# HGRN output from packed score blocks, and a new order of the scan's queues

## The reference, cut to what matters

```
diff = bi[..., :, None, :] - bi[..., None, :, :]
decay = jnp.exp(jnp.where(causal, diff, -jnp.inf))
scores = jnp.einsum("bhtd,bhsd,bhtsd->bhts", qi, ki, decay)
o = (jnp.einsum("bhts,bhsv->bhtv", scores, vi)
     + jnp.einsum("bhtd,bhdv->bhtv", qi * jnp.exp(bi), state))
```

## Time and profile before

| what | value |
|---|---|
| median of 3 executions | 1441.62 us (1437.52 to 1441.77) |
| the profiled execution | 1439.57 us, of which the span of its core is 1437.5 us |
| busy share of the span: PE, DVE, ACT, POOL | 97%, 70%, 48%, 14% |
| TensorE clock granted over the span | 0.988 of full |
| the scan | from 417.8 us to 575.9 us of the span |

### The profile page before, as it was taken

One profiled execution on the slowest core, in us unless ns is written; L12 is line 12 of the kernel. 1 busy time (PEld: TensorE's weight loads), 2 busy tenths in 40 slices (PEclk: granted clock), 3 DMA queues, 4 the chain that ended last, 5 costly groups with the idle time before them and its releaser, 6 DMA issues.

```text
span 1437.5 us, 22414 instructions
## 1 busy us (share of the span) xinstructions
PE 1398.9 (97%) x8579; PEld 1166.2 (81%) x8579; DVE 999.3 (70%) x1508; ACT 696.5 (48%) x1344; POOL 199.0 (14%) x225
## 2 busy tenths in 40 slices
PE   9999999999988888999999999999999999999998
PEld 7877888888877777878888888888888888888886
DVE  7584545561136777367897999999999575577567
ACT  6443456411366776256674343334444444454455
POOL 4000001101036655010000000000000144400000
PEclk9999999999998999999999999999999999999999
DMA  9642334446523433544442334335326766424213
GB/s 260 81 73 30 45 88 123 156 104 106 150 82 104 123 105 95 181 141 154 147 135 87 109 103 165 100 116 176 118 74 240 251 191 197 140 89 132 88 59 147
DMA packets 157866, 181.96 MB, mean 127 GB/s; under 512 B 25849, under 2 KB 96703, under 8 KB 157760
## 3 DMA queue, kind: packets, MB, share of 16 engines
q1 hardware_dynamic: 157760, 180.53, 43.3%
HBM read 130.43 MB, written 49.28 MB: 125 GB/s over the span
## 4 chain that ended last, share of the span: by engine, by line
PE 88%; DVE 4%; ACT 2%; DMA 2%; issue 2%; SPq 2%; DVEq 0%; ACTq 0%
PE psum L2538 9%; PE psum L2539 9%; PE psum L2540 9%; PE psum L2477 5%; PE psum L2479 5%; PE psum L2478 5%; PE psum L678 4%; PE psum L680 4%; PE psum L679 4%; PE psum L2450 4%; PE psum L2451 4%; PE psum L2452 4%; PE psum L736 3%; PE psum L738 3%; PE psum L737 3%; PE psum L1398 2%
## 5 line engine op out<-in xcount | busy, mean ns | idle before, releaser
L166 DVE TENSOR_TENSOR w_wlo<-w_raw,w_whi 128x1024 fp32r<-128x1024 f32 x66 | 87.8, 1332 | 231.9 <-ACT w_whi L151 231.7
L151 ACT ACTIVATE w_whi<-w_raw 128x1024 fp32r<-128x1024 f32 x66 | 69.7, 1059 | 177.0 <-PE psum L2452 80.2
L3271 DVE TENSOR_TENSOR g_slot<-w_raw,g_slot 128x512 fp32r<-128x512 f32 x77 | 62.5, 812 | 65.3 <-ACT g_slot L2845 65.3
L678 PE MATMUL psum<-h_hi,w_whi 128*128 128x512 f32 x256 | 100.7, 393 | 0.0
L680 PE MATMUL psum<-h_hi,w_wlo 128*128 128x512 f32 x256 | 99.7, 390 | 0.0
L679 PE MATMUL psum<-h_lo,w_whi 128*128 128x512 f32 x256 | 99.7, 389 | 0.0
L2845 ACT ACTIVATE g_slot<-w_raw 128x512 fp32r<-128x512 f32 x77 | 48.7, 632 | 104.8 <-PE psum L2479 99.6
L2450 PE MATMUL psum<-w_whi,m_hi 128*128 128x512 f32 x224 | 88.2, 394 | 0.9 <-DVE w_wlo L166 0.9
L2451 PE MATMUL psum<-w_wlo,m_hi 128*128 128x512 f32 x224 | 87.3, 390 | 0.0
L2452 PE MATMUL psum<-w_whi,m_lo 128*128 128x512 f32 x224 | 87.2, 389 | 0.0
L3529 POOL TENSOR_TENSOR mixed_home<-mixed_home 128x512 f32<-128x512 f32 x11 | 14.7, 1344 | 507.7 <-DMA mixed_home<-in_w_down 506.4
(11 more groups left out here) (463 smaller groups left out, 3883.1 us busy)
## 6 DMA issues: line engine op xcount, KB each, us to landing
w_raw<-in_w_up SPq DMA_DIRECT2D x39, 512.0 KB, 3.9
w_raw<-in_w_in SPq DMA_DIRECT2D x36, 512.0 KB, 6.3
s_rows<-pair_work SPq DMA_DIRECT2D x11, 1024.0 KB, 4.2
w_raw<-s_rows SPq DMA_DIRECT2D x44, 256.0 KB, 2.7
g_rows<-pair_work SPq DMA_DIRECT2D x18, 512.0 KB, 2.6
w_raw<-g_rows SPq DMA_DIRECT2D x33, 256.0 KB, 3.1
w_raw<-in_w_out SPq DMA_DIRECT2D x16, 512.0 KB, 4.5
mixed_home<-in_w_down SPq DMA_DIRECT2D x32, 256.0 KB, 3.4
```

Source lines behind the costliest of these rows:

```text
L678: pe.matmul(out, wh[:, w], self.hi[:, kt, part], start=(kt == 0), stop=False)
```

## The change

1. `s_h_scores`, the clearing of it, the second `s_h_near` buffer and `sp_unpack` with its 32 DMAs go. The HGRN output of a head is summed straight from the packed blocks: 4 products of 32 x 32 blocks on the diagonal, 2 of 32 x 32 blocks off it, 1 of a 64 x 64 block (`s_h_far`), and the product with the state as before.
2. The last level's decay is made like the others: one `dve_differ` (128 x 512) and two ACT exponentials, in place of eight small ones.
3. The order of all four queues is new. On PE, `pe_hgrn` of chunk c moves from the end of chunk c into the beginning of chunk c+1, `pe_solve` and `pe_outputs` move forward, score 7 moves behind `mix_g`, dt32 and dx. DVE, ACT and SP follow.
4. `hd` moves from bank 3 to bank 1, and `mix_g` from bank 2 to bank 7.

```diff
-    BANK_OF = {"ks": 2, "solve": 3, "gd": 3, "og": 4, "oh": 5, "hd": 3, "turn": 2, "mix_g": 2, "mix_h": 5,
+    BANK_OF = {"ks": 2, "solve": 3, "gd": 3, "og": 4, "oh": 5, "hd": 1, "turn": 2, "mix_g": 7, "mix_h": 5,
...
         out = self.banks.open(pe, ("oh", c), self.BANK_OF["oh"])
+        near, far = self.near_heads(), self.packed(self.far)
         for h in range(NH):
-            if c:
-                pe.matmul(hs(out, h), hs(self.hqd, h), hs(self.hstate, h), start=True, stop=False)
-            ins = pe.matmul(hs(out, h), hs(self.sc, h), hs(self.hv, h), start=(c == 0), stop=True)
-        self.multiplied.mark(ins, ("oh", c))
+            for b in range(P // SB):
+                rows = slice(b * SB, (b + 1) * SB)
+                ins = pe.matmul(hs(out, h)[rows, :], near[rows, h, 0:SB], hs(self.hv, h)[rows, :], start=(h == 0), stop=False,
+                                skip_group_check=True)
+        self.multiplied.mark(ins, ("oh", c, 0))
+        if c:
+            for h in range(NH):
+                pe.matmul(hs(out, h), hs(self.hqd, h), hs(self.hstate, h), start=False, stop=False, skip_group_check=True)
+        self.done(pe, ("oh", c, 0))
+        for h in range(NH):
+            for b in range(0, P // SB, 2):
+                keys, queries = slice(b * SB, (b + 1) * SB), slice((b + 1) * SB, (b + 2) * SB)
+                ins = pe.matmul(hs(out, h)[queries, :], near[keys, h, SB:2 * SB], hs(self.hv, h)[keys, :], start=False, stop=False,
+                                skip_group_check=True)
+        self.multiplied.mark(ins, ("oh", c, 1))
         if c < NT - 1:
             self.banks.released(pe, ("turn", c))
             self.pe_products(pe, ("hd", c), self.BANK_OF["hd"], lambda h: hs(self.hkd, h), lambda h: hs(self.hv, h))
+        self.done(pe, ("oh", c, 1))
+        for h in range(NH):
+            ins = pe.matmul(hs(out, h)[P // 2:P, :], far[0:P // 2, h, :], hs(self.hv, h)[0:P // 2, :], start=False,
+                            stop=(h == NH - 1), skip_group_check=True)
+        self.multiplied.mark(ins, ("oh", c))
...
         for c in range(NT):
             more = c + 1 < NT
+            if c:
+                self.pe_hgrn(pe, c - 1)
             self.pe_score(pe, c, 2)
             if c:
                 self.pe_dt64(pe, c)
             self.pe_score(pe, c, 3)
+            if c:
+                self.pe_solve(pe, c)
...
```

More of the change, by code:

```diff
@@ L1275, in __init__ @@
             self.ed, self.ql, self.kl = k.ed, k.ql, k.kl
-            self.sc, self.hqd, self.hkdt, self.hkd, self.hstate, self.hv = (
-                t("h_" + n) for n in ("scores", "qd", "kdt", "kd", "state", "v"))
+            self.sc_gap, self.hqd, self.hkdt, self.hkd, self.hstate, self.hv = (
+                t("h_" + n) for n in ("gap", "qd", "kdt", "kd", "state", "v"))
             self.gate = [t("h_gate"), t("g_gate")]
             self.on = t("normed", DM)
-            self.near = [t(f"h_near{i}", DG // 2) for i in range(2)]
-            self.middle = t("h_middle", NT * NH)
+            self.near, self.far = t("h_near", DG // 2), t("h_far", DG // 2)
             self.junk = t("junk", P, mybir.dt.bfloat16)
@@ L1307, in near_part, with near_heads @@
         return ap[:, at:at + NH * width].rearrange("p (h t) -> p h t", h=NH)
[L1309 to L1310 removed]
+    def near_heads(self):
+        return self.near[:].rearrange("p (h t) -> p h t", h=NH)
     def packed_blocks(self, ap, m):
@@ L1349, in load_rows @@
         sp.dma_start(tile[:], self.front.rows_out[c * P:(c + 1) * P, at:at + DG]).then_inc(self.s[name + "_in"], 16)
-    def sp_unpack(self, sp, c):
-        self.banks.released(sp, ("score", c, LEVELS - 1))
-        self.banks.released(sp, ("near", c))
-        if c:
[L1356 to L1360, removed]
     def sp(self, sp):
@@ L1534, in pe_hgrn @@
         pe.wait_ge(s["v_in"], (c + 1) * 16)
-        pe.wait_ge(s["unpacked"], (c + 1) * (P // SB) * 16)
-        self.banks.released(pe, ("score", c, LEVELS))
+        for n in (LEVELS - 1, LEVELS):
+            self.banks.released(pe, ("score", c, n))
+        self.banks.released(pe, ("near", c))
         if c:
@@ L1577, in pe @@
                 self.pe_dx(pe, c + 1)
-            self.pe_hgrn(pe, c)
+            self.pe_score(pe, c, 7)
+            if more:
+                self.pe_ks(pe, c + 1)
             self.pe_score(pe, c + 1, 0)
@@ L1602, in act_exp @@
         ed = self.ed[n % 3]
-        if lv in (0, LEVELS - 1) and n >= 3:
+        if lv == 0 and n >= 3:
             act.wait_ge(self.s["levels"], n - 2)
@@ L1608, in act_exp @@
                                  scale=-1.0, bias=1.0)
[L1609 to L1615, removed]
         else:
-            act.wait_ge(self.s["differed"], c * self.NEAR + lv)
+            act.wait_ge(self.s["differed"], c * (LEVELS - 1) + lv)
             act.activation(side(ed[:], 0), side(ed[:], 0), ACT.Exp, scale=-1.0)
@@ L1777, in dve_near @@
         self.done(dve, ("score", c, self.NEAR))
-        if c >= 2:
-            dve.wait_ge(self.s["unpacked"], (c - 1) * (P // SB) * 16)
-        bank, blocks = self.banks.of(("near", c)), self.near_heads(c)[:, :, 0:SB]
+        if c:
+            self.done(dve, ("oh", c - 1))
+        bank, blocks = self.banks.of(("near", c)), self.near_heads()[:, :, 0:SB]
         for n in range(self.NEAR + 1):
@@ L1800, in dve_place @@
         data = self.packed(self.banks.of(key))[0:P - ahead, :, 0:ahead]
[L1801 to L1806, removed]
+        if c:
+            self.done(dve, ("oh", c - 1))
+        here = self.packed(self.far)[0:ahead] if n == LEVELS else self.near_heads()[0:P - ahead, :, SB:2 * SB]
+        ins = dve.tensor_copy(here, data)
         self.banks.release(ins, key)
@@ L1887, in dve @@
         self.dve_rhs(dve, 0)
[L1888 to L1891, removed]
+        dve.memset(self.near[:], 0.0).then_inc(s["cleared"], 1)
         self.front.finished(dve)
@@ L1912, in dve @@
             self.dve_place(dve, c, 6)
+            if more:
+                self.dve_state(dve, c)
+            self.dve_query(dve, c)
             if c:
@@ L1916, in dve @@
                 self.slabs.remainder(dve, self.front.first["q"] + NH + 1)
[L1917 to L1921, removed]
             self.dve_dt(dve, c + 1, 0)
+            self.dve_dx(dve, c + 1)
             if c:
                 self.dve_mix(dve, c - 1, 1)
+            self.dve_differ(dve, c + 1, 2)
+            self.dve_place(dve, c, 7)
         self.dve_outputs(dve, NT - 1)
```

53 lines of the change are left out of this document (21 added, 32 removed).

## The result

The changed kernel takes 1468.03 us (median of 4, 1466.17 to 1470.11) against 1441.69 before: ratio 1.0189, 95% interval 1.0165 to 1.0214, slower by 26 us. The sign was forecast, the size was not: 12 us were predicted, and the time lies just above the range of 1438 to 1468 us.

A forecast was written before the change was run, and what follows sets the result against it. A ring of handoffs, not one full engine, was taken to bound the kernel. Six chunks +5.8, first -1.3, last +3.1, clock +4.5 gave +12.1 on 1441.62: 1453.7 us, range 1438 to 1468.

The forecast's parts named there:

- The ring: Handoffs between PE and DVE in each chunk: a DVE leg of 11.9 us plus a PE leg of 9.0 us.
- The products: HGRN output with hd on PE from packed blocks: diagonal tiles run at once, 4.95 us a chunk at full clock.
- the serial tiles: Rival: PE's diagonal tiles run one after another, +29 us over eight chunks, 1482 us; chance 0.10.
- The full-clock chunk: Each of six chunks takes 20.9 us against 19.94 before, +5.8 us in all.
- DVE's leg: From dt64's end on PE to DVE's release of mix_g: 11.9 us of handoff and DVE work per chunk.
- The clock term: PE's two idle times per chunk bring the lower clock in every second chunk, 1.5 us each: +4.5, between 0 and +9.
- The ends: First chunk -1.3 us, as its DMA wait goes; last chunk +3.1 us, 15.7 from dt64 to the end against 12.6.
- PE with its wait for y32 alone: Rival: bank 7 is free in time, a chunk is PE's own work plus 1.35 us, 19.3; 1439 us, chance 0.15.
- PE alone as the bound: Rival: PE has neither wait and stays at the upper clock, 17.9 us a chunk, 1429 us; chance 0.11.
- Part 2: Last level's decay as one DVE difference and two ACT exponentials: +0.65 us on DVE's path, ACT's saved 2 us bring nothing.

The follow-up runs named there:

- the bank number: The changed kernel with mix_g in bank 0 instead of bank 7, so score 7 need not wait for its release: 1444.66 us, ratio 1.0019.
- parts 1 and 2 in the old order: The kernel before with packed HGRN output and the last decay as one difference and two exponentials, queues and banks as before: 1433.46 us, ratio 0.9954.
- the gap filled: The changed kernel with mix_g's four transposes issued three times in chunks 1 to 6, occupying PE ahead of dt32: 1456.88 us, ratio 1.0118.
- the packed output alone: The kernel before with HGRN output from packed blocks and no unpacking DMAs, every queue and bank as before: 1432.36 us, ratio 0.9937.
- the new order without the difference: The changed kernel with mix_g in bank 0 and eight small ACT exponentials again in place of the DVE difference: 1443.18 us, ratio 1.0009.
- outputs first: The changed kernel with mix_g in bank 0 and DVE's outputs of the chunk before placed ahead of its HGRN state update: 1443.01 us, ratio 1.0011.

## Why the prediction was wrong, point by point

**The ring is right.** Where each chunk would wait, for whom and how long came as told: 1.7 us before score 7 for `mix_g`, about a microsecond before dt32, no wait for the unpacking DMAs. DVE's idle time before the copy of dt64 was 5.8 us, 3 forecast. That the bank clash makes the loss is shown by the bank number: without it the loss is gone. That the rest of the new order costs too is shown by parts 1 and 2 in the old order, 11 us below.

**The products are right.** 5.19 us measured at the full clock for the output with hd, 4.95 forecast, 8.5 for the serial tiles. The four 32 x 32 tiles on the diagonal do run at once with 128 columns and one bank:

```profile
461.32 1.08 PE L1531 MATMUL psum<-s_h_v,s_h_near 32*32 32x128 f32 x32
462.33 1.16 PE L1536 MATMUL psum<-s_h_state,s_h_qd 128*128 128x128 f32 x8
```

32 records in 1.01 us, and 0.9 was taken; one after another they would need 3.6 by the forecast's estimate. The rule on row tiles and banks of the Trainium skill ("TensorEngine Tiling (Array Packing)", "Restrictions and Gotchas") would have given that. The measurement decides against it for tiles that differ in row and column both.

**The full-clock chunk was sized 0.7 too short.** 20.9 forecast, 21.62 measured with the gap filled. I followed score 7's bank to its last user and not og's. Bank 4 is free only after DVE's outputs, which the new order puts behind the state update, so og, `mix_h` and score 6 come later, and DVE then waits 0.77 us for score 6, a wait that was not in its leg:

```profile
497.09 0.68 DVE L1766 TENSOR_TENSOR s_h_ed<-hgrn_f 128x512 f32<-128x512 f32 x1
498.55 0.29 DVE L1797 COPY s_h_near<-psum 96x128 f32<-96x128 f32 x1 [0.77 <-PE psum L1465]
```

DVE's leg with its handoff was 12.58 (490.50 to 503.08), 12.0 forecast; the output's 0.24 makes it 0.8, a little more than the 0.7 to be explained. Over six chunks 4.3 us.

**The clock term failed.** This is the step of the prediction that failed; the sizes of the ring above and of the ends below add to it. It took every second chunk at 1.5 us: +4.5, at most +9. From dt64 to dt64 the six chunks took 140.9 us, 23.5 each; less 21.62 that is 1.9 a chunk, 11 us. Every one of the six had a low stretch, and in the last three it was about twice as long (a clock of 0.85 and 0.86 over a chunk, and 0.93 and 0.94 in two of the others). Even the upper end allowed for one stretch per chunk like those of before, and no more. "Every second" was low by what lay on record, too: the forecast set one gap of 2.17 us that was not followed by the lower level against one of 3.10 that was, but another gap of 2.17 in the same trace was followed by it:

```profile
455.87 0.46 PE L1542 MATMUL psum<-s_h_state,s_h_qd 128*128 128x128 f32 x2 [2.17 <-DMA s_h_scores<-s_h_near]
...
457.34 0.63 PE L1542 MATMUL psum<-s_h_state,s_h_qd 128*128 128x128 f32 x2
```

Five of the six outputs from 455.87 to 555.40 had the lower level behind them (clock 0.90 to 0.92 up to the next output); five of six at 1.5 would have been +7.5. Why the stretches of the changed kernel are longer stays open. Two gaps stand close together there, and with the first one nearly filled the time fell by 11 us; but a gap of about a microsecond without the wait for `mix_g` is followed by the lower level as well, in five of six chunks of one kernel and in one of six of another. So it is open what sets the length.

**The ends.** First chunk -1.3 forecast, +0.9 measured (dt64 of chunk 1 ends at 444.53, 443.68 before, though the scan began 0.4 us earlier), with a low stretch of 13.7 us where before had two, of 6.8 and of 3.6. Last chunk +3.1 forecast, +7.6 measured. From the end of dt64 to the output projection it took 20.3 us where it took 12.6. og waited 2.73 us for bank 4 there, score 7 waited 1.66, and PE ran at the lower level between them:

```profile
590.64 0.77 PE L1504 MATMUL psum<-s_g_state,qkv 128*128 128x128 f32 x2 [2.73 <-DVE s_normed L1858]
...
598.45 0.65 PE L1465 MATMUL psum<-s_h_ql,s_h_kl 128*64 128x64 f32 x8 [1.66 <-DVE m_lo L1867]
```

Together 0.9 + 21.4 + 7.6 = 29.9, by which the output projection starts later in the span, against the forecast's 12.1. Of the excess of 17.8, 11.1 lie in the six chunks (4.3 the size of the ring, the rest the clock) and 6.7 at the two ends, where low stretches have their part again.

**The rivals.** Serial tiles: ruled out by the 1.01 us. PE with its wait for y32 alone (a chunk of 19.3): that is what the kernel with the bank number comes near to, at 20.0. PE alone as the bound: not in this order, but in the old order with the packed output, at 18.76.

**Part 2** was taken at +0.65 a chunk on DVE's leg and nothing on ACT. In the old order it cost 0.5 to 0.7.

## What to carry to other kernels

A table of buffers or banks is part of the order of the queues: when steps are moved, follow for every bank the last user and the engine that releases it, all of them and not only the one that catches the eye. Here one bank number made 23 us, and another bank's wait was overlooked. A wait of PE can cost more than its length, since the clock may fall behind it; count in the trace at hand how many waits are followed by the lower level before you put a share on it. When the times of one kernel fall into two groups, look at the groups and not at the median: here they were 6 us apart. Before a reordering is judged, time its parts alone: here the packed output alone was a gain of 9 us, and it was hidden under an order that, with its banks, cost 35.

## What the hardware showed that I had not expected

- More work made the kernel faster: 0.87 us of surplus transposes per chunk took 11 us off the changed kernel. Two chunks with waits alike to 0.1 us differ by 1.48 us, with a granted clock of 1.00 and 0.93.
- A single long gap of 1.04 or 1.05 us was followed by the lower level in five chunks of six (the new order without the difference), in three of six (outputs first) and in one of six (the bank number alone). What makes the difference no run here shows.
- A low stretch can last much longer than the gap that it follows: 17 us with PE busy for 24.37 of 24.62 us in the first chunk of the packed output alone (clock 0.65). By times and mean clocks, half of the executions of that same kernel seem to have gone without it. Similar or longer waits in other chunks were followed by shorter stretches, or none.
- Diagonal 32 x 32 tiles with 128 columns in one bank: 32 records in 1.01 us, as fast as eight records of 128 x 128 (1.09).
